# A two-layer hybrid backbone on one core: splits and a third diagonal buffer in the SSD pairs, value copies on VectorE between mLSTM heads, and a final norm applied tile by tile

## The chip, the cores and the metric

The kernel runs on one core of a Trainium2 chip. The time is that of one execution on the device, in microseconds. TensorE (PE) does matmuls and transposes, ScalarE (ACT) activations and copies, VectorE (DVE) elementwise work, scans and reductions, GpSimd (POOL) elementwise work and masks (affine selections), and SyncE (SP) issues DMAs. ScalarE issues some DMAs too. Each engine works off its own program in order, and engines meet through semaphores.

## The reference

One sample of 512 latent tokens and 256 context tokens, 1024 features, two layers, all in float32. Layer 0 runs gated linear attention (GLA, 4 heads) and Mamba-2 SSD (16 heads of 64 values, 128 states) beside each other; layer 1 runs a bidirectional mLSTM (4 heads of 512) in column-major grid order. Each layer ends with a SwiGLU FFN, and a final RMSNorm follows. Cut to what matters here:

```python
# SSD, both directions; per head h, chunks of 64, scalar decay
y, ... = bidir_scan(ch, bh * dt[0], bh * dt[1], xh, log_a[0], log_a[1], ...)
y = y + xh * d_skip ;  y = y * silu(z) ;  y = rmsnorm(y per group) ;  x += gate * (y @ w_out)

# mLSTM, per head and direction
s = einsum('bhid,bhjd->bhij', qc, kc) * exp(log_d - m_row)
num = einsum('bhij,bhje->bhie', s, vc) + w_inter * einsum('bhid,bhde->bhie', qc, c0)
h = num / max(abs(den), exp(-m_row))
hs = layernorm_nobias(h_f + flip(h_b)) ;  out = (hs + skip * xc) * silu(z)

# end
out = x * rsqrt(mean(x * x) + eps) * final_norm
```

## The kernel before

Activations lie transposed: `xT[P, 8, 768]` holds 8 tiles of 128 features by 768 tokens (512 latent, then 256 context; in layer 1 from the mLSTM on only the latent ones). A matmul of a weight tile with the activations is three matmuls of split float32 numbers, high times high, high times low, low times high. `weight_segments` orders all weight tiles in one line; they go through a ring of four buffers. SyncE loads a tile of 512 KB (`load`, L583), GpSimd splits it (`split`, L695 to L704) into `w_hi` and `w_lo`, TensorE multiplies (`tile_products`, L865; `project_unit`, L881), and `mm_done`, `evac` and `w_split` count the tiles. Results lie in PSUM: eight banks of 512 words, two of them a slot of 768.

*SSD stage* (around segments `out0` and `out1`). The 16 heads go in 8 pairs. For each head SyncE broadcasts two rows of cumulated decays to all partitions (`load_rows`, L618, a ring of two, 768 KB) and six rows for the context part. GpSimd selects the backward diagonal blocks into `Db` (L722; two buffers of 768 words, the one of head h is free when head h - 2 has been added up, `fb_done`), then the forward ones into `Dm` (L730; four buffers, two of them over `act_hi`). ScalarE takes exponentials (`decays_of`, `diagonal_decays`, `backward_decays`), and VectorE's `head_weights` (L2521) does, for head h: `exponents(h + 1)`, the context product `Dx` (L2550), the two sums of forward and backward blocks (L2533, L2536), the multiplication of `Dm` with the scores `cb` (L2539), and after an odd head the output of the pair before (L2556). TensorE's `pair_products` (L1184) multiplies the weights of two heads with the values; within it stands `context_decays` of the next odd head (L1160). Heads 0 to 7 use group 0's scores, heads 8 to 15 group 1's: TensorE computes seven pieces of them (`group_piece`, L1091), four ahead of pair 3's products and three behind them (L1213 to L1235), and ScalarE copies them to `cb` and `cbx` (`group_copy`, L1832) after head 8's decays, in the order of `SECOND` (L357). The first four weight tiles of `out1` are split by GpSimd after the selections of heads 5, 7, 9 and 11 (L733).

*mLSTM heads* (L1481 to L1537 on TensorE). In each head TensorE computes the outputs from `vt` and `Wf` (L1516), then the next head's stabiliser rows (`stabiliser_rows`, L1449) and values (`value`, L1432): four tiles of `xm`, each in two pieces of four and two 128x128 products, which go alternately to banks 2 and 3, so that piece i needs the copy of piece i - 2. Behind them stands the mean over features (L1526), then the next head's scores (`scores_of`, L1458). ScalarE copies the outputs to `hh`, takes the next head's exponentials (`weights`, L2066) and then copies the eight value pieces to `vt` (`head_value_copies`, L2054), with the load of the next `xm` tile behind each second one (ring of two). VectorE, meanwhile, adds the maxima (`weight_exponents`, L2740), sums `hh` over its four tiles (L2820, L2823) and waits for the mean (L2827).

*End.* Segment `down12` is the last: 8 tiles, each added to `xT` (L2482), squared by ScalarE (L1597) and summed (L2234). Then follow the sums over features (L814), the root (L1585), the reciprocal and a diagonal matrix (L2228, L2229), its spreading to all partitions by TensorE (L820), `fin` = x times `final_norm` times that (L2863, 8 instructions), 32 transposes into two banks (L1566), 8 copies to `obuf` (L2137), and four stores of 512 KB from ScalarE's queue (L2140), each as soon as its 128 tokens are complete.

## Time and profile before

| | |
|---|---|
| time, 3 runs | median 2545.46 us (2544.45 to 2546.82) |
| profiled execution | 2540.74 us, its span 2539.0 us |
| VectorE, ScalarE, GpSimd busy over the span | 56%, 25%, 42% |
| granted TensorE clock, mean | 0.966 of full |
| instructions | 33404 |

The profile page divides the span into 40 slices; in those of the SSD stage TensorE's busy share falls from 9 tenths to 7, and the granted clock with it:

```
PE   5999999999877989999999989999998999999997
PEclk8999999999888999999999999999999999999999
```

One slice is 63.5 us, so slices 11 to 13, where the shares are lower, are 635 to 825 us. A timeline row gives the start in the span, the duration, engine, line, operation, destination and sources, and in brackets how long the engine idled before it and who released it. Matmuls in float32 appear as two instructions each. The mLSTM heads lie between 1796 and 2105 us, the end from 2490 us on.

### The profile page before, as it was taken

How to read it: one execution, taken by the hardware profiler on the slowest of the kernel's cores; microseconds unless marked ns; L12 is line 12 of the kernel's file. 1: busy time of each engine (PE TensorE's matmuls, PEld its weight loads, DVE VectorE, ACT ScalarE, POOL GpSimd, SP SyncE). 2: the span in 40 equal slices, each digit the busy share in tenths (PEclk: the TensorE clock that was granted, in tenths of full speed). 3: DMA queues.
4: the chain of work that ended last, by engine and by line, in shares of the span. 5: the costliest groups of instructions: out<-in, count | busy, mean ns of one | idle time of the engine just before them, and what ended most of it. 6: DMA issues, size and time to landing. Idle time of an engine off the chain costs nothing.

```text
span 2539.0 us, 33404 instructions
## 1 busy us (share of the span) xinstructions
PE 2377.8 (94%) x12133; PEld 1882.9 (74%) x12133; DVE 1426.8 (56%) x2455; ACT 635.4 (25%) x1042; POOL 1073.3 (42%) x815
## 2 busy tenths in 40 slices
PE   5999999999877989999999989999998999999997
PEld 3887888887534878888888878876555457888886
DVE  4574778775586257778886646644366555111113
ACT  3202354433684131000000133133312302201001
POOL 2362343344362424464454344444211034666663
PEclk8999999999888999999999999999999999999999
DMA  7652342354430234343444213354233112333332
GB/s 273 216 175 83 98 144 73 116 173 150 163 114 13 84 66 117 100 133 102 129 117 116 79 46 122 122 164 141 75 96 108 35 53 83 97 94 99 92 95 71
DMA packets 390135, 280.98 MB, mean 111 GB/s; under 512 B 31106, under 2 KB 355228, under 8 KB 390012
## 3 DMA queue, kind: packets, MB, share of 16 engines
q1 hardware_dynamic: 333644, 201.51, 27.2%
q10 hardware_dynamic: 56368, 77.81, 9.0%
q8 instruction: 80, 1.31, 0.2%
q14 instruction: 43, 0.35, 0.0%
HBM read 237.21 MB, written 42.07 MB: 110 GB/s over the span
## 4 chain that ended last, share of the span: by engine, by line
PE 60%; DVE 5%; ACT 2%; issue 1%; DMA 1%; POOL 1%; DVEq 0%; ACTq 0%; POOLq 0%; SPq 0%
PE PS L869 43%; PE PS L1516 3%; PE PS L1359 3%; PE PS L1371 3%; PE PS L1468 2%; PE PS L820 1%; PE PS L1442 1%; DVE xcr L2300 1%; PE PS L1427 1%; PE PS L814 1%; PE PS L878 1%; DMA xmr<-xm_d 1%; PE PS L1314 0%; DVE hh L2851 0%; DMA w_raw<-in_ffn_w 0%
## 5 line engine op out<-in xcount | busy, mean ns | idle before, releaser
L700 POOL TENSOR_TENSOR w_hi<-w_raw,ones 128x128 fp32r<-128x128 f32 x244 | 160.9, 659 | 1269.2 <-DMA w_raw<-in_ffn_w 438.3
L703 POOL TENSOR_TENSOR w_lo<-w_raw,w_hi 128x1024 fp32r<-128x1024 f32 (+1 forms) x244 | 590.1, 2419 | 20.4
L869 PE MATMUL PS<-act_hi,w_hi 128*128 128x512 f32 (+1 forms) x1824 | 540.7, 362 | 29.1 <-DVE act_lo L2259 11.5
L869 PE MATMUL PS<-act_hi,w_lo 128*128 128x512 f32 (+1 forms) x1824 | 524.7, 353 | 0.0
L869 PE MATMUL PS<-act_lo,w_hi 128*128 128x512 f32 (+1 forms) x1824 | 521.4, 352 | 0.0
L869 PEld LDWEIGHTS PS<-act_hi,w_hi 128*128 128x128 f32 x1824 | 297.3, 192 | 78.5 <-issue 24.2
L869 PEld LDWEIGHTS PS<-act_lo,w_hi 128*128 128x128 f32 x1824 | 295.5, 191 | 48.3
L869 PEld LDWEIGHTS PS<-act_hi,w_lo 128*128 128x128 f32 x1824 | 295.5, 191 | 47.0
L2202 DVE SCALAR_TENSOR_TENSOR mf_acc<-mf_ring,cs,mf_acc 128x128 f32<-128x128 f32 x784 | 268.1, 417 | 2.0
L701 POOL TENSOR_SCALAR w_hi<-w_raw 128x896 fp32r<-128x896 f32 (+1 forms) x244 | 246.1, 1009 | 0.0
L2482 DVE SCALAR_TENSOR_TENSOR xT<-PS,modv,xT 128x512 f32<-128x512 f32 (+1 forms) x120 | 74.9, 657 | 236.2 <-PE PS L869 208.8
L2611 DVE TENSOR_TENSOR fhp<-fsg,PS 128x768 f32<-128x768 f32 (+1 forms) x44 | 36.1, 821 | 237.1 <-PE PS L869 211.5
L869 PE MATMUL PS<-hid_hi,w_hi 128*128 128x512 f32 (+1 forms) x528 | 163.2, 363 | 0.0
L869 PE MATMUL PS<-hid_hi,w_lo 128*128 128x512 f32 (+1 forms) x528 | 160.8, 359 | 0.0
L869 PE MATMUL PS<-hid_lo,w_hi 128*128 128x512 f32 (+1 forms) x528 | 160.5, 358 | 0.0
L1949 ACT ACTIVATE fsg<-PS 128x768 f32<-128x768 f32 (+1 forms) x44 | 31.1, 707 | 423.9 <-PE PS L869 423.8
L943 PE MATMUL PS<-act_hi,w_hi 128*128 128x512 f32 x448 | 121.6, 352 | 0.7 <-ACT stage L1708 0.7
L943 PE MATMUL PS<-act_hi,w_lo 128*128 128x512 f32 x448 | 116.4, 341 | 0.0
L943 PE MATMUL PS<-act_lo,w_hi 128*128 128x512 f32 x448 | 115.8, 340 | 0.0
L1952 ACT ACTIVATE hid_hi<-fhp 128x768 f32 (+1 forms) x44 | 32.6, 741 | 298.2 <-DVE fhp L2611 298.2
L869 PEld LDWEIGHTS PS<-hid_lo,w_hi 128*128 128x128 f32 x528 | 87.3, 188 | 16.4
L869 PEld LDWEIGHTS PS<-hid_hi,w_lo 128*128 128x128 f32 x528 | 87.4, 189 | 16.1
(348 smaller groups left out, 3605.1 us busy)
## 6 DMA issues: line engine op xcount, KB each, us to landing
w_raw<-in_ffn_w SPq DMA_DIRECT2D x120, 512.0 KB, 3.9
mf_ring<-in_w_mod SPq DMA_DIRECT2D x56, 512.0 KB, 4.0
w_raw<-in_a_w_in SPq DMA_DIRECT2D x44, 512.0 KB, 4.0
proj<-stage ACTq DMA_DIRECT2D x44, 384.0 KB, 4.0
w_raw<-in_b_w_up SPq DMA_DIRECT2D x32, 512.0 KB, 4.6
m_ring<-in_w_mod SPq DMA_DIRECT2D x12, 1024.0 KB, 8.2
rows<-g_d SPq DMA_DIRECT2D x16, 768.0 KB
m_raw<-in_w_mod SPq DMA_DIRECT2D x4, 2048.0 KB, 12.6
```

Source lines behind the costliest of these rows:

```text
L700: pool.tensor_tensor(w_hi[:, s, 0], w_raw[:, s, 0], ones[:], ALU.mult)
L701: pool.tensor_scalar(w_hi[:, s, 1:kt], w_raw[:, s, 1:kt], 1.0, 1.0, ALU.mult, ALU.mult).then_inc(w_hi_done, 1)
L703: pool.tensor_tensor(w_lo[:, s, 0:kt], w_raw[:, s, 0:kt], w_hi[:, s, 0:kt].bitcast(F32), ALU.subtract).then_inc(w_split, 1)
L869: last = pe.matmul(to[:, c0:c1], w[:, s, k, :], x[:, k, c0:c1], start=k == 0 and w is w_hi and x is hi, stop=k == kt - 1 and w is w_lo)
L943: last = pe.matmul(slot((n + 1) % 2)[:, c0:c1], w[:, n % RING, k, :], x[:, k, c0:c1], start=k == 0 and w is w_hi and x is act_hi, stop=k = ...
L1359: last = pe.matmul(bank(Z_BANK[j]), w[:, j % RING, k, :], x[:, k, 0:LAT], start=k == 0 and w is w_hi and x is act_hi, stop=k == KD - 1 and ...
L1371: last = pe.matmul(out, w[:, s, k, :], head_act(x, h, t), start=k == 0 and w is w_hi and x is act_hi, stop=k == KD - 1 and w is w_lo)
L1468: last = pe.matmul(bank(SCORE_BANKS[i]), xch[:, t, c * P:c * P + P], qp[:, t], start=t == 0, stop=t == 3)
L1516: last = pe.matmul(bank(OUT_BANKS[t]), vt[:, c, t * P:t * P + P], Wf[:, c], start=i == 0, stop=i == 5)
L2202: ins = dve.scalar_tensor_tensor(acc, mf_ring[:, s % 2, k], c, acc, ALU.mult, ALU.add)
L2482: ins = dve.scalar_tensor_tensor(x, y, g, x, ALU.mult, ALU.add)
L2611: dve.tensor_tensor(fhp[:, i, 0:n], fsg[:, i, 0:n], slot(s)[:, 0:n], ALU.mult).then_inc(evac, 2)
```

## The change

In the SSD stage: `Db` gets a third buffer, over `act_hi`; the backward selection of head h waits for head h - 3, and that of head 2 for out0's last product. The four splits go to heads 1, 2 and 3. All seven pieces of group 1 stand ahead of pair 3's products, in a new order. In the mLSTM stage: VectorE copies the values of heads 1 to 3, one tile ahead of its sums over `hh` and three behind them, and ScalarE's loads of `xm` move into `weights`. At the end: the weights of `final_norm` are multiplied in as each tile is done, half of the transposes stand behind tile 5 of `down12`, the reciprocal root is applied as a scale per token after the transposes, by ScalarE to the second half and by VectorE to the first, and SyncE issues the stores. New semaphore names lie on old semaphores. The diff, cut:

```diff
-        SECOND = (0, 1, 4, 5, 2, 3, 6)
+        SECOND = (0, 1, 4, 5, 6, 2, 3)
-        Db = sb("Db", [P, 2, T], offset=30720)
+        Db = [sb(f"Db{i}", [P, T], offset=30720 + 4 * T * i) for i in range(2)]
+        Db += [nc.alloc_sbuf_tensor_at("Db2", [P, T], F32, offset=act_hi_at + 8 * DM)]
...
-        fin = sb("fin", [P, KD, LAT], offset=24576)
-        obuf = sb("obuf", [P, 4, D], offset=43008)
+        fin = nc.alloc_sbuf_tensor_at("fin", [P, KD, LAT], F32, offset=zst_at)
+        obuf = nc.alloc_sbuf_tensor_at("obuf", [P, 4, D], F32, offset=act_hi_at)
@@ SyncE, at its end
+            for t in range(4):
+                sp.wait_ge(out_put, 5 + t)
+                sp.wait_ge(half_scaled, HALF0 + t + 1)
+                sp.dma_start(out[0, t * P:t * P + P, :], obuf[:, t]).then_inc(out_st[t % 2], 16)
@@ GpSimd
-                        if h >= 2:
-                            pool.wait_ge(fb_done, h - 1)
-                        pool.affine_select(out=diagonals(Db[:, h % 2], 0, 6, P), ...
+                        if h == 2:
+                            pool.wait_ge(mm_done, n0)
+                        elif h >= 3:
+                            pool.wait_ge(fb_done, h - 2)
+                        pool.affine_select(out=diagonals(Db[h % 3][:], 0, 6, P), ...
-                        if h == 2:
-                            pool.wait_ge(mm_done, n0)
...
-                        if h in (5, 7, 9, 11):
-                            split(n0 // RING, (h - 5) // 2, kt)
+                        if h in (1, 2, 3):
+                            for s in ((0, 1), (2,), (3,))[h - 1]:
+                                split(n0 // RING, s, kt)
@@ TensorE
+                    if name == "down12":
+                        last_tiles(name, kt, hi, lo, n, ready, ready0)
+                        return
...
+            def last_tiles(name, kt, hi, lo, n, ready, ready0):
+                r = segs[name][0] // RING + 1
+                for s in range(RING):
+                    project_unit(name, r, s, kt, hi, lo, n, ready, ready0)
+                    if s == 1:
+                        final_transposes(0, (0, 1, 2, 3))
...
                 if p == 3:
-                    for i in SECOND[0:4]:
+                    for i in SECOND:
                         group_piece(1, i)
...
                 elif p == 3:
-                    pair_products(p)
-                    for i in SECOND[4:7]:
-                        group_piece(1, i)
-                    context_decays(8)
+                    pair_products(p, lambda: context_decays(8))
...
+            def final_transposes(half, quarters):
+                pe.wait_ge(fin_ready, 4 * half + quarters[-1] + 1)
+                if half:
+                    pe.wait_ge(out_put, 4)
+                for t in range(4):
+                    for q in quarters:
+                        last = pe.transpose(bank(1 + 2 * t)[:, q * P:q * P + P], fin[:, 4 * half + q, t * P:t * P + P], ident[:])
+                    if quarters[-1] == 3:
+                        last.then_inc(out_tr, 1)
...
+            final_transposes(1, (0, 1, 2))
             pe.wait_ge(evac, segs["end"][0])
-            rstd_products(nacc, LAT, 3)
...
+            rstd_sums(nacc, LAT, 3)
+            final_transposes(1, (3,))
@@ ScalarE
+                    if name == "final" and k == 4:
+                        for t in range(4):
+                            act.wait_ge(out_tr, t + 1)
+                            act.activation(obuf[:, t, 0:512], bank(1 + 2 * t), ACT.Copy).then_inc(out_put, 1)
...
+            def next_xm(h, t):
+                if h and 4 * h + t + 2 < 16:
+                    act.wait_ge(qv_mm, QV_MM0 + 12 * h + 6 + 2 * t)
+                    load_xm(4 * h + t + 2)
@@ ScalarE, weights(h): next_xm(h, d) behind each direction's exponentials, next_xm(h, 2), next_xm(h, 3) at its end
...
                     weights(h + 1)
-                    head_value_copies(h + 1)
...
+            act.wait_ge(diag_done, rstds[0])
+            for t in range(4):
+                act.wait_ge(out_tr, 5 + t)
+                act.activation(obuf[:, t, 512:1024], bank(1 + 2 * t), ACT.Copy, scale=rcol[:, 0, t:t + 1]).then_inc(out_put, 1)
@@ VectorE
+            def final_weight(k):
+                dve.wait_ge(evac, segs["down12"][0] + k + 1)
+                dve.tensor_scalar(fin[:, k], xT[:, k, 0:LAT], par("final_norm", k), None, ALU.mult).then_inc(fin_ready, 1)
...
+            def value_copies(h, t):
+                f = 12 * h + 4 + 2 * t
+                for c0, c1 in ((0, 4), (4, 6)):
+                    dve.wait_ge(qv_mm, QV_MM0 + f + 1)
+                    dve.tensor_copy(vt[:, c0:c1, t * P:t * P + P], bank(2 + f % 2, ...)...).then_inc(val_put, 1)
+                    f += 1
...
                     weight_exponents(h + 1)
+                    value_copies(h + 1, 0)
...
                 dve.drain().then_inc(hs_rdy, 1)
+                if h + 1 < ML_HEADS:
+                    for t in range(1, 4):
+                        value_copies(h + 1, t)
                 dve.wait_ge(mean_mm, h + 1)
...
-            norm_sums("final", LAT)
-            for k in range(KD):
-                dve.scalar_tensor_tensor(fin[:, k], xT[:, k, 0:LAT], par("final_norm", k), slot(3)[:, 0:LAT], ALU.mult, ALU.mult).then_inc(fin_ready, 1)
+            add_norm_square(NORMS.index("final"), KD - 1, LAT)
+            dve.drain().then_inc(sum_done, 1)
+            final_weight(KD - 1)
+            rstds[0] += 1
+            dve.wait_ge(std_done, rstds[0])
+            dve.reciprocal(rcol[:, 0, 0:4], rcol[:, 0, 0:4]).then_inc(diag_done, 1)
+            dve.wait_ge(diag_done, rstds[0])
+            for t in range(4):
+                dve.wait_ge(out_put, t + 1)
+                dve.tensor_scalar(obuf[:, t, 0:512], obuf[:, t, 0:512], rcol[:, 0, t:t + 1], None, ALU.mult).then_inc(half_scaled, 1)
```

## Rows read from the trace of the kernel before

**Rows 1.** The page, busy time of TensorE: us, share of the span, instructions.
```profile
PE 2377.8 (94%) x12133; PEld 1882.9 (74%) x12133; DVE 1426.8 (56%) x2455; ACT 635.4 (25%) x1042; POOL 1073.3 (42%) x815
```

**Rows 2.** Waits of TensorE: who waited for whom, us in total, times, longest.
```profile
PE PS L1442 <- ACT vt L2060: 14.4, 3, 4.8
```

**Rows 3.** Timeline, from mLSTM head 0 to head 1: TensorE and VectorE.
```profile
1820.17 1.98 PE L1456 MATMUL PS<-negM,ident 8*128 8x512 f32 x4
1822.08 1.60 PE L1442 MATMUL PS<-bdv,xmr 128*128 128x128 f32 x12
1822.19 0.69 DVE L2746 TENSOR_TENSOR Wb<-PS,ucol 128x512 f32<-128x512 f32 x1 [0.17 <-PE PS L1456]
1823.51 1.73 DVE L2823 TENSOR_TENSOR mtmp<-mtmp,hh 128x512 f32<-128x512 f32 x2
1828.48 5.73 PE L1442 MATMUL PS<-bdv,xmr 128*128 128x128 f32 x24 [4.79 <-ACT vt L2060]
1835.90 1.02 PE L1526 MATMUL PS<-mtmp,ones 128*128 128x512 f32 x2
1836.96 2.87 DVE L2827 SCALAR_TENSOR_TENSOR hh<-PS,hh 128x512 f32<-128x512 f32 x4 [11.72 <-PE PS L1526]
```

**Rows 4.** Busy time by engine in one SSD pair, clock and DMA share.
```profile
701.25:717.39 16.14, 12.15 (x48) 4.78 (x48) 15.28 (x12) 12.82 (x37) 13.55 (x10) 0.90 0.38 125
```

**Rows 5.** Timeline of the end: last residual, sums, a last transpose group, copies, stores.
```profile
2516.52 0.75 DVE L2482 SCALAR_TENSOR_TENSOR xT<-PS,modv,xT 128x512 f32<-128x512 f32 x1 [2.85 <-PE PS L869]
2518.93 1.02 PE L814 MATMUL PS<-ones,nacc 128*128 128x1 f32 x8 [2.52 <-DVEq L2240]
2531.47 0.35 ACTq L2140 DMA_DIRECT2D out_y<-obuf  x1
2532.62 0.63 PE L1566 MATMUL PS<-ident,fin 128*128 128x128 f32 x4 [0.40 <-ACT obuf L2137]
2534.84 0.34 ACTq L2140 DMA_DIRECT2D out_y<-obuf  x1
```

**Rows 6.** DMA traffic from 2500 to 2540 us, one number for each us.
```profile
GB/s 22 242 130 0 0 0 0 0 0 0 0 0 0 0 0 0 0 0 0 0 16 0 0 0 0 0 0 0 0 0 0 0 283 401 385 418 406 213 0 0
```

**Rows 7.** VectorE's copies out of PSUM at line 2156: ns least, median, most.
```profile
L2156 DVE COPY xT<-PS x12: 691/692/693, 18.6 to 27.1; 128x512 f32<-128x512 f32 x12
```

**Rows 8.** Timeline of the SSD pairs, VectorE, GpSimd, ScalarE and TensorE.
```profile
701.08 2.83 DVE L2539 TENSOR_TENSOR Dm<-Dm,cb 128x2560 f32<-128x2560 f32 x1
707.44 2.68 POOL L703 TENSOR_TENSOR w_lo<-w_raw,w_hi 128x1024 fp32r<-128x1024 f32 x1
707.82 2.59 DVE L2536 TENSOR_TENSOR Dm<-Dm,Db 128x256 f32<-128x256 f32 x1
710.44 2.83 DVE L2539 TENSOR_TENSOR Dm<-Dm,cb 128x2560 f32<-128x2560 f32 x1
710.61 3.37 POOL L722 TENSOR_SCALAR_AFFINE_SELECT Db<-rows 128x768 f32<-128x768 f32 x1 [0.50 <-DVE Dm L2536]
714.02 0.70 ACT L1869 ACTIVATE Db<-Db,nb 128x128 f32<-128x128 f32 x2 [3.32 <-POOL Db L722]
714.02 1.10 DVE L2519 TENSOR_TENSOR Db<-Db,nb 128x512 f32<-128x512 f32 x1 [0.76 <-POOL Db L722]
719.36 1.45 PE L1191 MATMUL PS<-xt,skip 128*128 128x512 f32 x4
728.07 0.60 ACT L1840 ACTIVATE cb<-PS 128x512 f32<-128x512 f32 x1 [5.17 <-PE PS L1111]
730.52 2.83 DVE L2539 TENSOR_TENSOR Dm<-Dm,cb 128x2560 f32<-128x2560 f32 x1 [7.22 <-ACT cbx L1840]
753.77 2.83 DVE L2539 TENSOR_TENSOR Dm<-Dm,cb 128x2560 f32<-128x2560 f32 x1
760.54 2.83 DVE L2539 TENSOR_TENSOR Dm<-Dm,cb 128x2560 f32<-128x2560 f32 x1
767.03 2.82 DVE L2539 TENSOR_TENSOR Dm<-Dm,cb 128x2560 f32<-128x2560 f32 x1
```

68 lines of the change are left out of this document (37 added, 31 removed).

## The prediction

> **What bounds the kernel now.** I read the page's busy shares first, then the waits by engine, then time-ordered instructions of the three places that the diff touches. TensorE is busy for 94% of the span [rows 1], so a wait costs time where it stops TensorE, or where it moves what TensorE gets next. The three places differ.
>
> In the mLSTM stage TensorE waits for ScalarE's copies of the value products three times, 14.4 us together [rows 2]. One turn from head to head is in [rows 3]: the stabiliser rows start at 1820.17, the first two value products at 1822.08, the third at 1828.48 after 4.79 us of idling, the mean product at 1835.90. It takes 15.7 us. The reader is to see that ScalarE was not slow: it works off the next head's exponentials first, because they stand ahead of the copies in its program.
>
> In the SSD pair loop TensorE is the idle one. In the 16.14 us of one pair VectorE is busy for 15.28, ScalarE for 12.82, GpSimd for 13.55 [rows 4]. So the loop runs at VectorE's pace, and what lengthens VectorE's own instructions counts.
>
> At the end TensorE has nothing left: from the last residual at 2516.52 to the end of the span, 22.5 us, a serial chain runs: sums, root, reciprocal, spreading, eight products for `fin`, transposes, eight copies, four stores [rows 5].
>
> **The end of the program.** Now: the last store is issued at 2534.84 and the span ends at 2539.0, so 4.2 us after it. The four stores of 512 KB are one stream at about 400 GB/s, from about 2532.3 to 2537.5 [rows 6]: 5.2 us, begun 0.9 us behind the first issue at 2531.47, and 1.5 us follow it.
> After: the weights of `final_norm` go on tile by tile (VectorE idles 2.85 us before each residual [rows 5], and one such product is under 0.75 us: hidden), the first half's 16 transposes stand behind tile 5, and the reciprocal root is applied at the very end as a scale. Four transposes take 0.63 us in the last row of that kind [rows 5], so 16 of them put about 2.2 us (16/4 x 0.63 = 2.5, less the tails that overlap) into the stage that TensorE bounds. ScalarE's four copies of half 0 lie beside tile 6. From the last residual on, in the old clock: 12 transposes (1.6 us) lie in the wait for the last square; sums at 2518.93 and root as before; reciprocal done at about 2520.5; the last four transposes run beside the root. Then ScalarE's four scaled copies at about 0.55 us each (such a copy shows 0.60 [rows 8], back to back a little less, an estimate), VectorE's four multiplications beside them: stores issued from 2521.3 to 2522.9. The stream then sets the end: 2521.3 + 0.9 + 5.2 + 1.5 = 2528.9. With the 2.2 us that is 2531.1, against 2539.0: **-8 us**. It cannot be below -11 (the spread product, `fin` and half of the copies are all there is to take), nor above -5, where the four stores from SyncE would come one by one at their 4.2 us latency in part. Moving the stores from ScalarE's queue to SyncE's puts them behind weight loads only, and DMA is almost silent from 2503 to 2531 [rows 6].
>
> **The turn between mLSTM heads.** ScalarE loses 24 copies, VectorE gets them. The only price of such a copy on VectorE is the copy of 128x512 out of PSUM at the start of the program, 0.69 us [rows 7]; that of 128x256 I estimate at 0.4. Counted from the stabiliser rows' start: value products 0 and 1 end at 3.5 (1.60 us for twelve instructions, 0.133 each; a pair of pieces is those twelve [rows 3]). VectorE finishes the second diagonal block at 2.7 and copies at 3.1 and 3.8, until 4.2. TensorE does pieces 2 and 3 from 3.8 to 5.4. VectorE now does its three sums over `hh`, 2.4 us (0.7, and 1.73 for two [rows 3]), until 6.6; the next copies come behind them, until 7.8. Pieces 4 and 5: 7.4 to 9.0. Copies until 9.7, pieces 6 and 7 until 11.0, mean product at 11.0. Now it is 15.7, so 4.7 less.
> Two loads of `xm` are moved: the one for piece 6 is issued after the second group of exponentials, about 6 us from the start, and has 3.4 us until piece 6; I take off 0.2 for a load that comes late: 4.5 a turn, three turns: **-13.5 us**. VectorE's 4.4 us of copies cover themselves: it idles 11.72 us before the mean now [rows 3]. Behind the mean product everything keeps its distance: scores wait for the last copy, which ends while the mean product runs. From both sides: with no copy late, TensorE's own work is 1.9 + 4 x 1.6 = 8.3 us, a gain of 7.4 a turn; if each pair waits for a full round of VectorE behind its sums, 2.
>
> **The SSD pairs.** Four edits have one answer, VectorE's time per head. The multiplications of `Dm` by `cb` are its beat [rows 8]. Without a weight split on GpSimd the beat is 6.77 us (753.77 to 760.54) and 6.49 (760.54 to 767.03); with one it is 9.36 (701.08 to 710.44). In that pair the sum of the short diagonal block, L2536, took 2.59 us where it lay against the split's 2.68 us: it ended 0.3 us behind it. So a split costs 2.6 us.
> *Splits.* Those at heads 5, 7 and 11 each cost 2.6, the one at head 9 fell into VectorE's wait of 7.22 us for `cb` [rows 8] and cost nothing. At heads 1 to 3 they meet out0's last tiles, where TensorE bounds, and the wait for head 4's rows; one of them may put head 3's selection back by some tenths, but head 4's rows arrive no sooner for that. So -7.8.
> *Third buffer.* ScalarE waits 3.32 us in a split pair for the even head's backward selection, VectorE 0.76 [rows 8]. The selection took 3.37 us because it started right with a multiplication of 2.83. With a third buffer it may start a head earlier. But without the splits ScalarE's own 12.8 us per pair [rows 4] and VectorE's 12.5 (13.26 less such a wait) are all but equal, so the pair goes from 13.26 to about 12.8: 0.45 x 5 pairs, -2.2. It cannot gain more than the 0.76 a pair, 3.8.
> *Second group.* Now TensorE goes into pair 3 at 719.36 and computes the last three pieces behind it; ScalarE waits 5.17 us for them and VectorE then 7.22 for the copies [rows 8]. After, TensorE waits before pair 3 for ScalarE's first copy (about 2 us), does the three pieces, and pair 3 starts some 5 us late against its head. `cb` is there 4 us sooner, but head 9's context product now stands behind pair 3 on TensorE, and VectorE waits for that instead: of the gain, nothing reaches head 9's multiplication, and I put this edit at +1.2 (pair 3's products take TensorE from 719.36 to about 727, 7.6 us, and with transposes and the context product behind them they end that much later than ScalarE's chain would). From -4 to +4.
> Also the second head's backward selection now waits for out0's last product, since its buffer lies over `act_hi`; the forward one, behind it, ends later by one selection, and ScalarE asks for it about then: 0 to +0.7, I take 0.
> Sum, with 0.8 for VectorE instructions that meet a selection at new places: -7.8 - 2.2 + 1.2 + 0.8 = **-8 us**, between -2 and -14.
>
> A rule of the Trainium skill speaks against this part. The row first: L2536 stood still until the split was done, and L722 until the multiplication was [rows 8]. The Trainium skill, "SBUF — State Buffer", section "Who interferes with whom", says that a VectorE instruction with two SBUF inputs and a GpSimd instruction that reads SBUF exclude each other, and whichever is second blocks. The trace agrees. By that rule a selection that may start when its rows land, and not with a multiplication, blocks VectorE where it used to be the one blocked: rival (a) below, which gives 2524 where the rows of the undisturbed pair give 2516.
>
> **The sum.** -8 - 13.5 - 8 = -29.5 us. The profiled execution took 2540.74 us (span 2539.0 and 1.7 around it), so 2511.2. The median of the three timed runs is 2545.46, 4.7 above it; I carry the difference over to the median: **2516.0 us**.
>
> **Rivals.**
> (a) The shared port takes back the third buffer and more. For: every selection now may start beside VectorE's short sums; the part of L722 outside the multiplication is 0.7 us [rows 8], and with the two forward ones that is some 2 us a head. At 0.8 us a head more in the ten heads from 5 on: +8, SSD at 0, total -21.5, 2524. Against: in the pair without a split such meetings cost only 0.3 us. 15%.
> (b) VectorE becomes the bound of the turn: its sums and drain are ahead of six of eight copies. If each turn gains 2 us and not 4.5: -22, 2523.5. For: the chain above has TensorE idle twice, 2.0 and 0.4 us. Against: the idle 11.72. 12%.
> (c) More comes: SSD -13 (the wait of 7.22 is saved in whole) and turns at -5.5: 2508. 10%.
> (d) Slower. TensorE's granted clock. In the pair loop it is 0.90 of full on average [rows 4], so part of that stretch ran at 1.2 GHz and not at 2.4, and TensorE idles there between products. If the value stage of a turn (three short bursts with idle between, in place of one long wait) left it at 1.2 for 12 us of full-speed work behind it, these would take 24, 36 more in three turns: -29.5 + 36 = +6.5, 2552. It decides from 30 us of such work. Against: the idle time there gets shorter in all. 2%.
> (e) The change does not do what it says: the third buffer's selection still waits, now for its rows (the ring of two row buffers is unchanged), and the reordering cancels: SSD -5, 2519; within my forecast's own range. 9%.
> My forecast has 52%.
>
> **How the numbers follow.** The time is that of the forecast. The range for 8 in 10 reaches to (a) and (b) and most of (c): 2509 to 2526. A measurement of this kernel tells about 0.2%, 5 us, from no change: faster by more than that has every case but (d) and some accident of code loading or order: 0.94, same 0.03, slower 0.03.
>
> **What would show it.** Turns: ScalarE as the releaser of value products gone, stabiliser row to mean product 11.2 us. End: the last store issued 6 to 7 us after the last residual, not 18; 16 transposes ahead of tile 6. SSD: the beat 6.0 to 6.8 in all heads from 4 on but 8 and 9, L2536 never at 2.6, no wait of 7 us before head 8's multiplication but one of 3 to 4 us on a context product of head 9. Wrong would be: a beat still near 9, a turn above 13.5, or TensorE's clock at half for long in either stage.

## The result and the profile after

The changed kernel takes 2509.8 us in the median of 4 runs (2505.1 to 2518.9), the one before 2545.0 in as many runs beside it (2541.9 to 2546.8): ratio 0.9876, 95% interval 0.9841 to 0.9911. The forecast was 2516.0. The profiled execution took 2505.09 us, its span 2503.4, 35.6 less than the profiled one before; the forecast made against that one was 29.5 less. One run of one experiment (two_buffers) took 9134.6 us, at a granted clock of 1.00 and for a reason that no trace shows, and is left out of that kernel's median and ratio.

TensorE is as busy as it was [rows 1]:

```profile
PE 2354.4 (94%) x12131; PEld 1869.7 (75%) x12131; DVE 1446.5 (58%) x2482; ACT 622.7 (25%) x1018; POOL 1053.7 (42%) x815
```

**The turns.** Waits of TensorE: who waited for whom, total, times, longest. in the three turns ScalarE is gone as releaser of value products [rows 2], and VectorE stands there with half of the time:

```profile
PE PS L1482 <- DVE vt L2804: 7.5, 9, 1.6
PE PS L828 <- DVEq L2895: 3.2, 1, 3.2
PE PS L1482 <- DMA xmr<-xm_d: 0.9, 1, 0.9
```

The same turn as in [rows 3], timeline of TensorE and VectorE in the changed kernel:

```profile
1804.83 1.98 PE L1496 MATMUL PS<-negM,ident 8*128 8x512 f32 x4
1806.74 1.60 PE L1482 MATMUL PS<-bdv,xmr 128*128 128x128 f32 x12
1807.93 1.02 DVE L2804 COPY vt<-PS 128x512 f32<-128x512 f32 x2 [0.40 <-PE PS L1482]
1808.77 1.58 PE L1482 MATMUL PS<-bdv,xmr 128*128 128x128 f32 x12 [0.43 <-DVE vt L2804]
1808.87 0.68 DVE L2879 TENSOR_TENSOR mtmp<-hh 128x512 f32<-128x512 f32 x1
1809.59 1.42 DVE L2882 TENSOR_TENSOR mtmp<-mtmp,hh 128x512 f32<-128x512 f32 x2
1811.15 1.02 DVE L2804 COPY vt<-PS 128x512 f32<-128x512 f32 x2
1811.98 1.58 PE L1482 MATMUL PS<-bdv,xmr 128*128 128x128 f32 x12 [1.64 <-DVE vt L2804]
1813.99 1.58 PE L1482 MATMUL PS<-bdv,xmr 128*128 128x128 f32 x12 [0.43 <-DVE vt L2804]
1815.40 1.02 PE L1572 MATMUL PS<-mtmp,ones 128*128 128x512 f32 x2
```

From the stabiliser rows to the mean product it is 1815.40 - 1804.83 = 10.57 us, and the same in the other two turns; before it was 15.73, 15.59 and 15.60. So 15.2 us in three turns. The listed waits fell by only 6.9 us (14.4 to 7.5), since a row that joins many products hides the short pauses between them: the 24 products at 1828.48 in [rows 3] take 5.73 us, where twelve take 1.60, so 2.5 us of pauses lie inside that row.

**The end.** Timeline from the first half's transposes on:

```profile
2480.46 1.91 PE L1300 MATMUL PS<-ident,fin 128*128 128x128 f32 x16
2480.66 0.75 DVE L2527 SCALAR_TENSOR_TENSOR xT<-PS,modv,xT 128x512 f32<-128x512 f32 x1 [2.19 <-PE PS L893]
2486.61 0.75 DVE L2527 SCALAR_TENSOR_TENSOR xT<-PS,modv,xT 128x512 f32<-128x512 f32 x1 [4.08 <-PE PS L893]
2490.82 0.75 DVE L2527 SCALAR_TENSOR_TENSOR xT<-PS,modv,xT 128x512 f32<-128x512 f32 x1 [2.33 <-PE PS L893]
2493.22 1.02 PE L828 MATMUL PS<-ones,nacc 128*128 128x1 f32 x8 [1.14 <-DVEq L2924]
2494.11 0.64 PE L1300 MATMUL PS<-ident,fin 128*128 128x128 f32 x4
2494.79 2.42 ACT L2187 ACTIVATE obuf<-PS,rcol 128x512 f32<-128x512 f32 x4 [0.24 <-DVE rcol L2928]
2494.80 1.68 DVE L2932 TENSOR_SCALAR obuf<-obuf,rcol 128x512 f32<-128x512 f32 x4
2495.51 2.90 SPq L682 DMA_DIRECT2D out_y<-obuf  x4
```

From the last residual to the end of the span 2503.4 - 2490.82 = 12.6 us, where it was 22.5 [rows 5]. DMA traffic from 2463 to 2503 us shows the stores at the same 400 GB/s as before [rows 6]:

```profile
GB/s 0 94 306 305 81 0 138 253 2 0 118 252 23 0 0 0 0 0 0 0 0 0 0 0 16 0 0 0 0 0 0 0 0 258 414 397 393 406 225 12
```

**The SSD pairs.** One pair by engine, as in [rows 4] (us, then PE, PEld, DVE, ACT, POOL busy, clock, DMA share, GB/s):

```profile
695.47:708.63 13.16, 9.50 (x45) 3.81 (x45) 12.30 (x11) 12.77 (x38) 6.80 (x6) 1.00 0.50 154
```

It takes 13.16 us where it took 16.14, and GpSimd has half of its work gone. Timeline rows that answer to [rows 8]:

```profile
671.09 2.67 POOL L716 TENSOR_TENSOR w_lo<-w_raw,w_hi 128x1024 fp32r<-128x1024 f32 x1
671.47 2.58 DVE L2587 TENSOR_TENSOR Dm<-Dm,Db 128x256 f32<-128x256 f32 x1
689.09 2.83 DVE L2590 TENSOR_TENSOR Dm<-Dm,cb 128x2560 f32<-128x2560 f32 x1
690.04 2.59 POOL L737 TENSOR_SCALAR_AFFINE_SELECT Db<-rows 128x768 f32<-128x768 f32 x1 [7.32 <-DMA xrow<-cross_d]
692.67 0.69 DVE L2570 TENSOR_TENSOR Db<-Db,nb 128x512 f32<-128x512 f32 x1 [0.76 <-POOL Db L737]
714.00 1.15 PE L1141 MATMUL PS<-rdiag,bct 128*128 128x512 f32 x2 [1.96 <-ACT cb L1882]
714.96 3.58 PE L1135 MATMUL PS<-rdiag,bct 128*128 128x512 f32 x4
719.30 2.83 DVE L2590 TENSOR_TENSOR Dm<-Dm,cb 128x2560 f32<-128x2560 f32 x1 [4.78 <-ACT cb L1882]
728.30 1.23 DVE L2601 TENSOR_TENSOR Dx<-PS,cbx 128x1024 f32<-128x1024 f32 x1 [4.09 <-PE PS L1195]
730.62 2.83 DVE L2590 TENSOR_TENSOR Dm<-Dm,cb 128x2560 f32<-128x2560 f32 x1
736.90 0.93 POOL L737 TENSOR_SCALAR_AFFINE_SELECT Db<-rows 128x768 f32<-128x768 f32 x1 [7.19 <-DMA xrow<-cross_d]
737.14 3.36 DVE L2590 TENSOR_TENSOR Dm<-Dm,cb 128x2560 f32<-128x2560 f32 x1
```

The reader is to see five things. The split now holds L2587 up at head 2. The backward selection of head 6 waits for a transfer (the last of its rows), starts inside the multiplication of head 4, and VectorE waits the same 0.76 us for it as before. And head 8's multiplication waits 4.8 us in place of 7.2, while head 9 then waits 4.1 us for its context product. Ahead of both, four products of group 1's pieces take 3.58 us behind TensorE's wait of 1.96, where the same four take 1.98 in six_last at a granted clock of 1.00; here it was 0.50 from 715 to 717 us. And the backward selection of head 12 starts 0.24 us ahead of the multiplication of head 10, which then takes 3.36 us in place of 2.83.

### The profile page after: what moved, and what is told of

Read it like the earlier page. It is cut to its first block, busy times and chain, and to the rows that moved or that the text cites. A ratio compares the mean times of both kernels' runs of the same rounds, so it can differ in the third digit from the quotient of the medians.

```text
span 2503.4 us, 33402 instructions
## 1 busy us (share of the span) xinstructions
PE 2354.4 (94%) x12131; PEld 1869.7 (75%) x12131; DVE 1446.5 (58%) x2482; ACT 622.7 (25%) x1018; POOL 1053.7 (42%) x815
## 4 chain that ended last, share of the span: by engine, by line
PE 60%; DVE 6%; issue 1%; POOL 1%; DMA 1%; ACT 1%; ACTq 0%; DVEq 0%; POOLq 0%; SPq 0%
PE PS L893 44%; PE PS L1562 3%; PE PS L1391 3%; PE PS L1403 3%; PE PS L1514 2%; PE PS L834 1%; PE PS L1482 1%; PE PS L828 1%; PE PS L1463 1%; PE PS L902 1%; DVE xcr L2345 1%; PE PS L1346 0%; DVE hh L2913 0%; DVE hh L2911 0%; PE PS L1222 0%
## 5 line engine op out<-in xcount | busy, mean ns | idle before, releaser
L713 POOL TENSOR_TENSOR w_hi<-w_raw,ones 128x128 fp32r<-128x128 f32 x244 | 151.6, 621 | 1264.0 <-DMA w_raw<-in_ffn_w 451.2
L893 PE MATMUL PS<-act_hi,w_hi 128*128 128x512 f32 (+1 forms) x1824 | 539.0, 361 | 26.6 <-DVE act_lo L2304 11.0
L893 PEld LDWEIGHTS PS<-act_hi,w_hi 128*128 128x128 f32 x1824 | 296.1, 192 | 75.7 <-issue 21.5
## 6 DMA issues: line engine op xcount, KB each, us to landing
m_raw<-in_w_mod SPq DMA_DIRECT2D x4, 2048.0 KB, 12.4
```

What stands on the lines that cost most here:

```text
L713: pool.tensor_tensor(w_hi[:, s, 0], w_raw[:, s, 0], ones[:], ALU.mult)
L893: last = pe.matmul(to[:, c0:c1], w[:, s, k, :], x[:, k, c0:c1], start=k == 0 and w is w_hi and x is hi, stop=k == kt - 1 and w is w_lo)
```

## The experiments

Times of stages come from each run's own profile, one for each kernel. The ratios of the experiments are to the kernel before as it ran beside each group of experiments (medians of 2542.0 to 2543.1 us), not to the 2545.0 of the first line. For SSD the yardstick is the distance from the start of head 1's multiplication by `cb` to that of head 15's. Heads 7 to 9 hold the switch to group 1.

| kernel | time, median (runs) | ratio, 95% interval | heads 1-15 | 3-7 | 7-9 | 9-15 |
|---|---|---|---|---|---|---|
| before | 2545.0 (4) | | 117.9 | 32.3 | 20.4 | 41.2 |
| changed | 2509.8 (4) | 0.9876 (0.9841 to 0.9911) | 111.6 | 26.1 | 22.0 | 38.3 |
| changed, again | 2508.3 (6) | 0.9868 (0.9839 to 0.9897) | 114.1 | 26.4 | 22.0 | 40.4 |
| splits_only | 2530.5 (10) | 0.9955 (0.9939 to 0.9972) | 111.4 | 26.3 | 21.5 | 38.1 |
| end_only | 2533.5 (10) | 0.9970 (0.9953 to 0.9986) | 117.7 | 32.3 | 20.4 | 41.2 |
| turns_only | 2529.3 (7) | 0.9941 (0.9924 to 0.9959) | 117.9 | 32.3 | 20.4 | 41.2 |
| two_buffers | 2503.0 (3) | 0.9850 (0.9800 to 0.9900) | 111.3 | 26.6 | 21.9 | 38.1 |
| late_splits | 2516.2 (4) | 0.9877 (0.9831 to 0.9924) | 117.5 | 32.8 | 18.8 | 40.8 |
| old_group | 2512.6 (4) | 0.9874 (0.9832 to 0.9916) | 114.1 | 28.3 | 22.3 | 38.1 |
| six_last | 2510.6 (4) | 0.9872 (0.9843 to 0.9900) | 110.8 | 26.2 | 19.1 | 40.4 |
| six_last_ctx | 2506.9 (4) | 0.9849 (0.9818 to 0.9879) | 107.5 | 26.4 | 15.9 | 39.8 |
| early_rows | 2510.6 (6) | 0.9869 (0.9839 to 0.9899) | 109.3 | 26.7 | 20.5 | 38.6 |
| combo | 2504.8 (6) | 0.9858 (0.9829 to 0.9887) | 107.4 | 26.4 | 15.9 | 39.8 |
| combo_two | 2505.6 (6) | 0.9860 (0.9831 to 0.9888) | 105.8 | 26.3 | 15.8 | 39.8 |

**two_buffers.** Undoes the third buffer.

```diff
-        Db += [nc.alloc_sbuf_tensor_at("Db2", [P, T], F32, offset=act_hi_at + 8 * DM)]
...
+                        if h >= 2:
+                            pool.wait_ge(fb_done, h - 1)
...
-                        elif h >= 3:
-                            pool.wait_ge(fb_done, h - 2)
   (every Db[h % 3] is Db[h % 2]; the wait for mm_done is back behind the backward selection)
```

> The changed kernel with two backward buffers in place of three (the wait for the head before the last is back). Yardstick of all runs on the SSD stage: from the start of head 1's multiplication by cb to that of head 15's, 117.9 us before the change, 111.6 after. Theory A (the forecast on record): the third buffer is worth 0.45 us a pair, so 113.8. Theory B: it is worth nothing, because a backward selection waits for its rows, and their load waits for ScalarE, which must have read the rows of two heads earlier: 111.6 +- 0.5, and the selections of heads 6 to 12 start at the same distance from the multiplications as in the changed kernel. Theory C: it costs (selections now lie against VectorE's short sums): 110.5 or less.

Measured 111.3, so the size is that of theory B: the third buffer is worth nothing (heads 3 to 15 take 86.6 us without it and 86.5 with it). Its mechanism is only half right. The first row is the backward selection of head 6, the others group its 16 selections by what ended the idle time before them (us, times):

```profile
689.76 3.38 POOL L734 TENSOR_SCALAR_AFFINE_SELECT Db<-rows 128x768 f32<-128x768 f32 x1 [2.01 <-DVE Dm L2586]
...
  DMA xrow<-cross_d: 32.5, 10
  DVE Dm L2586: 10.3, 6
```

With two buffers six selections wait for VectorE's sum and not for rows. They start 0.2 us behind the start of the multiplication that follows the sum. With three, those of heads 6 to 9 start 0.4 to 1.7 us into it, when the rows are there. Both end behind it. Later the third buffer does let some go sooner: those of heads 12, 13 and 15 start 0.1 to 0.35 us ahead of a multiplication, and the multiplications of heads 10, 11 and 13 then take 3.36, 3.36 and 3.47 us in place of 2.83 [the last two rows above]. So they save VectorE one wait of 0.76 us and four stretched `exponents` (0.95 us in place of 0.69), and cost it 1.7. With two buffers one multiplication is so stretched, by 0.5 us (head 1).

**late_splits.** Undoes the move of the splits.

```diff
-                        if h in (1, 2, 3):
-                            for s in ((0, 1), (2,), (3,))[h - 1]:
-                                split(n0 // RING, s, kt)
+                        if h in (5, 7, 9, 11):
+                            split(n0 // RING, (h - 5) // 2, kt)
```

> The changed kernel with the four weight splits of out1 back behind the selections of heads 5, 7, 9 and 11. Theory A: each of three costs 2.6 us again and the early places cost nothing: 111.6 + 7.8 = 119.4. Theory B: three cost 2.6 each, but the early places cost 1.2 (heads 1 to 3 took 25.2 us from head 1's multiplication to head 3's, 24.0 before): 118.2. Theory C: with three buffers a split is hidden in part, since the selection behind it can wait: 115 or less.

117.5: the splits cost 5.9 of the yardstick, nearest to theory B (118.2) and against C. The two stretches with splits take 32.8 and 40.8 us, as before the change; the third buffer hides none of it. Heads 1 to 3 take 25.1 us here too, so the early splits alone do not explain the 1.2 us more that heads 1 to 3 show after the change; splits_only, which has them and nothing else, takes 25.5 there. Heads 7 to 9 take 18.8 us here against 20.4 in the kernel before, which has the same splits: with the splits late, the new order gains 1.6. A split now meets another instruction, to the same price, here `exponents`:

```profile
692.93 2.88 DVE L2569 TENSOR_TENSOR Db<-Db,nb 128x512 f32<-128x512 f32 x1
...
692.91 2.35 POOL L716 TENSOR_TENSOR w_lo<-w_raw,w_hi 128x1024 fp32r<-128x1024 f32 x1
```

**old_group.** Undoes the order of group 1.

```diff
-        SECOND = (0, 1, 4, 5, 6, 2, 3)
+        SECOND = (0, 1, 4, 5, 2, 3, 6)
...
-                    for i in SECOND:
+                    for i in SECOND[0:4]:
                         group_piece(1, i)
...
-                    pair_products(p, lambda: context_decays(8))
+                    pair_products(p)
+                    for i in SECOND[4:7]:
+                        group_piece(1, i)
+                    context_decays(8)
```

> The changed kernel with the old handling of group 1's scores: four pieces ahead of pair 3's products, three and both context products behind. Theory A: the new order costs 1.2 us: 110.4. Theory B, from the two traces: head 7's to head 9's multiplication took 22.0 us after the change and 20.4 before, so 1.6 less: 110.0. Theory C: the new order gains, and the loss is from the missing cover of the split at head 9: 112 or more.

114.1 would speak for theory C, but the 2.2 us more lie at heads 3 to 7, ahead of the edit, where TensorE's clock was low for longer in this run (last section). Heads 7 to 9, where the edit is, take 22.3 us against 22.0: the order of the change is worth 0.3, neither A's nor B's loss. Inside, head 8 comes 3.9 us sooner with the new order (10.7 behind head 7, against 14.6) and head 9 3.6 later (11.3 behind head 8, against 7.7). One thing stands in the way of this comparison: in the changed kernel the four products behind TensorE's wait of 1.96 us ran at a low clock and took 1.6 us longer [the row at 714.96 above]. In early_rows below, which has the new order and not this drop, heads 7 to 9 take 20.5. And splits_only shows 1.1 us of loss there with the old order. So theory C is right in part: the loss at heads 7 to 9 goes with the missing cover for the split at head 9.

**splits_only.** The kernel before, with the splits moved and nothing else (the edit of late_splits, reversed).

> The kernel before, with only the four splits moved to heads 1, 2 and 3. Theory A: 117.9 - 7.8 = 110.1. Theory B: 117.9 - 8.4 (the beats of the three heads fell from 9.35 to 6.5) + 1.2 for the early places = 110.7, that is 0.9 us less than with the whole SSD part, because the rest of that part costs. Theory C: without the third buffer the even heads' selections still wait for VectorE, and only half comes: 114. The whole time falls by the same amount: 2538 by A and B.

111.4: the splits alone give all of the SSD gain, 6.5 us, though not all of theory B's 7.2. Heads 3 to 7 and 9 to 15 gain 9.0, heads 7 to 9 give 1.1 back and heads 1 to 3 1.5. Head 8 waits for its scores still longer than before [rows 8]:

```profile
723.73 2.83 DVE L2540 TENSOR_TENSOR Dm<-Dm,cb 128x2560 f32<-128x2560 f32 x1 [8.50 <-ACT cbx L1841]
```

**end_only** and **turns_only.** The kernel before, with one part of the change each, word for word: for end_only `last_tiles`, `final_transposes`, `final_weight`, the scaled copies and the stores from SyncE; for turns_only `value_copies`, `next_xm` and the waits on `val_put`.

> The kernel before, with the end-of-program part alone. Theory A (the forecast): from the last residual to the end of the span 12.4 us where it was 22.5, 16 transposes of 2.2 us ahead of tile 6, so -8 in all, about 2535 in the median. Theory B: the gain needs nothing of the other parts, and the profile shows the same 12.6 and 2.2 as the whole change. Theory C: a part of it is lost in the rest of the program (the final transposes hold up the last weight tiles' products further): -5, 2538.

2533.5, ratio 0.9970: 7.6 us, theories A and B. From the last residual (2517.89) to the end of the span (2529.6) it is 11.7 us, 0.9 less than in the whole change: the first store is issued 4.7 us behind the residual in both, and the stores end sooner here.

> The kernel before, with VectorE's value copies in the mLSTM turns alone. Theory A (the forecast): each turn takes 11.2 us from stabiliser rows to mean product, -13.5 in all. Theory B, from the trace of the changed kernel: 10.6 each, -15.2, about 2528; and where GpSimd's split behind head 3 meets VectorE's third sum of squares, 2.1 us of that are lost again (the wait of TensorE for the sum is 3.2 us in place of 1.1). Theory C: the turns only show a gain that heads 1 to 3 pay back (scores wait for the last copies): the distance from one mean product to the next falls by less than 5 us.

2529.3, ratio 0.9941: 15.0 us. The turns take 10.57 us each, and the wait for the sum of squares behind head 3 is 3.1 us: theory B. C's number is met and its reason is not: from one mean product to the next it is 80.4 and 81.9 us, 84.2 and 85.0 before, so 3.8 and 3.1 less. Between the first two TensorE's clock was 0.91 in one window of 20 us (1854 to 1874), where it was 1.00 at the same instructions of the whole change (1838 to 1858), and between the others it waited 1.8 us once for a sum of VectorE's, as it does in end_only, which has the old turns. In the first profile of the whole change the same distances are 79.0 and 79.9, so 5.2 and 5.1 less, and nothing is paid back; in the second they are 78.9 and 81.8. In the nine profiles with turns of 10.57 us the two distances add up to 158.9 to 164.1 us, 161.3 in the mean, in the three with the old turns to 168.8 to 172.0, 170.0 in the mean. So of the 10.0 us that two turns gain 8.7 are seen in the mean; that heads 1 to 3 never pay back is not shown.

The three ratios of single parts multiply to 0.9867; the whole change measured 0.9876 and 0.9868. The parts add up within their intervals of about 0.0016 each, and the third buffer and the new order, which no single part has, need not add anything.

**six_last.** The changed kernel, with `SECOND` as before and all seven pieces ahead of pair 3.

```diff
-        SECOND = (0, 1, 4, 5, 6, 2, 3)
+        SECOND = (0, 1, 4, 5, 2, 3, 6)
```

> The changed kernel with the old order of group 1's pieces (0, 1, 4, 5, 2, 3, 6), all seven still ahead of pair 3's products. In the changed kernel piece 6 stands ahead of 2 and 3 and waits 1.96 us for ScalarE's first copy, and these two behind it. Theory A: the order costs as much as that wait: head 8's multiplication and pair 3's products come 2.2 us earlier, and head 15's too; from head 1's to head 15's multiplication 109.4 us in place of 111.6. Theory B: pieces 2 and 3 wait for VectorE's output of pair 2 instead, at about the same time, and nothing changes: 111.6. Theory C: head 8 comes earlier, but ScalarE or GpSimd bound heads 9 to 15 and take it back: head 8 -2, head 15 within 0.5.

Head 8 comes 2.3 us sooner and heads 7 to 9 take 2.9 us less, theory A's mechanism; the piece that stands third from the end waits 0.33 us for VectorE in place of 1.96 for ScalarE, and its four products take 1.98 us, at full clock, where they took 3.58. Part of the 2.9 us is therefore the clock. The low clock followed the wait in three of the four profiles that have it (1.96 us), and in the five that have these products and not the wait they took 1.88 to 1.99 us:

```profile
711.55 1.98 PE L1135 MATMUL PS<-rdiag,bct 128*128 128x512 f32 x4 [0.33 <-DVE yT L2607]
714.23 1.45 PE L1215 MATMUL PS<-xt,skip 128*128 128x512 f32 x4
```

The yardstick shows 110.8 and not 109.4: heads 9 to 15 took 40.4 us, two more than in the first run of the changed kernel and as many as in its second. Theory C is not excluded by this run; the next one speaks against it.

**six_last_ctx.** In addition the context product of head 9 moves into pair 3's products.

```diff
                         between()
+                    if p == 3 and c == 3:
+                        context_decays(9)
...
-                if p == 3:
-                    context_decays(9)
```

> As six_last, and head 9's context product stands within pair 3's products, behind their fourth chunk, in place of behind the transposes that follow them. VectorE waited 4.1 us for it in the changed kernel. Theory A: VectorE's wait goes, head 9's multiplication follows ScalarE's exponentials at 6.5 to 7 us behind head 8's in place of 11.3, ScalarE's wait for pair 3 bounds head 10, and head 1 to head 15 takes 105 to 106. Theory B: the product waits for VectorE's context product of head 8 and holds up pair 3's last chunks, so head 10 comes as late as before: 109.4, as in six_last.

107.5, between A and B: VectorE's wait for the product is 0.3 us where it was 4.1 [the row at 728.30 above], and head 9 follows head 8 by 7.5 us in place of 11.3. Then head 10 needs 8.5, for pair 3's products end late against it (ScalarE waits 1.80 us for them), which is B's mechanism in part.

```profile
726.58 0.70 PE L1195 MATMUL PS<-xrow 6*128 6x512 f32 x2 [0.66 <-DVE Dx L2601]
```

**early_rows.** The memory of the third buffer goes to a third buffer of backward rows, with transfers of their own.

```diff
+        row_b = nc.alloc_sbuf_tensor_at("row_b", [P, T], F32, offset=act_hi_at + 8 * DM)
...
-                        sp.dma_start(rows[:, h % 2], src).then_inc(rows_in[h % 2], 16)
+                        sp.dma_start(rows[:, h % 2, 0], src).then_inc(rows_in[h % 2], 16)
...
+                        if h >= 4 and h + 1 < SSD_HEADS:
+                            load_back(h + 1)
...
-                        pool.wait_ge(rows_in[h % 2], ROWS_IN0 + 32 * (h // 2 + 1))
+                        pool.wait_ge(rb_in[RB[h]], back_count(h))
```

> The changed kernel with two backward buffers, and the memory of the third given to a third buffer for the backward rows, loaded by a transfer of their own one head ahead, so that a backward selection no longer waits for its rows. Theory A: the rows are what holds the selections; VectorE's wait of 0.76 us in every pair goes, and the beats of a pair fall from 13.2 us to ScalarE's 12.8: from head 1's to head 15's multiplication 109 to 110 us in place of 111.3. Theory B: the selections already come as soon as they help, and nothing changes: 111.3 +- 0.4. Theory C: selections that start early meet VectorE's short sums, or block the forward ones: 112 or more.

109.3, the size of theory A and not its mechanism. The pairs take as long as before: 26.7 us from head 3 to 7. Now ten selections wait for VectorE's sum, as in this row of head 7, and VectorE still waits 0.76 us in five of the pairs:

```profile
694.04 3.38 POOL L756 TENSOR_SCALAR_AFFINE_SELECT Db<-rows 128x768 f32<-128x768 f32 x1 [1.40 <-DVE Dm L2610]
...
713.76 1.88 PE L1157 MATMUL PS<-rdiag,bct 128*128 128x512 f32 x4
```

The 2 us come from head 3, which follows head 2 by 6.9 us in place of 8.3, and from heads 7 to 9 (20.5 us against 21.9 in two_buffers). The latter is the clock: the four products behind TensorE's wait of 1.97 us take 1.88 us here and 3.34 in two_buffers, where the granted clock was 0.50 from 717 to 719 us. So the selection is held twice: by its rows, and, about 1 us earlier, by the sum, which stands right ahead of the multiplication. One buffer more of either kind moves it only from one to the other. Both at once were not tried.

**combo** and **combo_two.** six_last_ctx with VectorE's sums set between its copies; combo_two with two buffers in addition.

```diff
                 for t in (2, 3):
+                    if h + 1 < ML_HEADS:
+                        value_copies(h + 1, t - 1)
                     dve.wait_ge(h_put, H_PUT0 + 4 * h + t + 1)
                     chain(dve.tensor_tensor(acc, acc, hh[:, t], ALU.add))
...
-                    for t in range(1, 4):
-                        value_copies(h + 1, t)
+                    value_copies(h + 1, 3)
```

> six_last_ctx with VectorE's sums over hh set between its value copies in the mLSTM turns (copy tile 0, sum, copy tile 1, sum, copy tile 2, sum, copy tile 3). Theory A: TensorE's wait of 1.64 us before the fifth piece goes, the last tile of xm, issued by ScalarE behind its exponentials, bounds pieces 6 and 7: a turn takes 9.3 us in place of 10.57, -3.8 in all. Theory B: it takes 8.8, since the transfer is in time. Theory C: the mean product, which needs the last sum, becomes the bound: 10.2. With SSD at 107.5 (as six_last_ctx) the span is some 7 to 8 us under the changed kernel's.

> combo with two backward buffers. If the third buffer is worth nothing here too: SSD 107.5 +- 0.5, the time that of combo. If the shorter SSD stage makes it useful: 108.5 to 110.

The turn takes 10.17 us: 0.4 less, a miss against A and B, and nearest to C's number, but not for C's reason. The transfer of `xm` is the next wait, and it comes for the third tile already:

```profile
1811.47 1.60 PE L1482 MATMUL PS<-bdv,xmr 128*128 128x128 f32 x12 [1.14 <-DMA xmr<-xm_d]
1813.57 1.58 PE L1482 MATMUL PS<-bdv,xmr 128*128 128x128 f32 x12 [0.50 <-DVE vt L2804]
```

SSD takes 107.4 and, with two buffers, 105.8, which is 1.2 less than was expected at least. The difference lies at heads 1 to 3 (25.4 and 23.9 us; why is not settled), and heads 3 to 15 take 82.0 in both: the third buffer is worth nothing here either. Both kernels have a lower median than the changed one (2504.8 and 2505.6 against 2508.3 beside them), but with six runs each from 2500.6 to 2514.2 the order among the three is not shown.

**after_again.** The changed kernel, unchanged.

> The changed kernel once more, unchanged, beside the others on one chip. All theories: about 2508 to 2510 in the median; SSD 111.6 +- 0.5 if TensorE's granted clock takes the same course, up to 3 more if it stays low longer; turns 10.57 each; 12.6 us from the last residual to the end. It tells what one profiled execution differs from another.

2508.3; the turns 10.57 each, the end 12.6. SSD 114.1, that is 2.5 more than the first time, within what was expected for a clock that stays low longer. It is the measure of how far two profiles of one kernel differ there.

## Why the prediction was right, point by point

Forecast 2516.0, measured 2509.8: inside the range of 2509 to 2526, 0.8 us above its lower end. Rival (c)'s 2508 is nearer than the forecast, but its reasons did not come: head 8's wait was not saved in whole, SSD gained 6.9 us and not 13, and a turn 5.1, between the 4.5 of the forecast and the 5.5 of (c). That the sum of the parts came out so close is in part luck, since errors of both signs lie in it.

**The end: right, and in its steps.** Forecast 12.4 us from the last residual to the end, measured 12.6; forecast 2.2 us for 16 transposes, measured 1.75 (the residual of tile 6 follows that of tile 5 by 5.95 us, that of tile 7 by 4.21, and end_only shows the same). The issues of the four stores lie from 4.7 to 7.6 us after the residual (2495.51 and 2.90 for the four; forecast 4.8 to 6.4), and the stream of four at 400 GB/s sets the end as forecast. Net -8.1 for -8.

**The turns: right mechanism, the size a little low.** Forecast 11.2 us a turn, measured 10.57. Pieces 2 and 3 started 3.94 us after the rows' start (forecast 3.8), 4 and 5 at 7.15 (7.4), 6 and 7 at 9.16 (9.4 by the forecast's steps), the mean product at 10.57 (11.0, and 0.2 for a late load). The terms mis-sized are VectorE's sums, 2.14 us and not 2.4, and its copies: two in 1.02, not 0.7 and 0.4 one after the other. Gain 15.2 for 13.5. Rival (b) falls: no turn gained only 2.

**SSD: the sum nearly right, from terms that were not.** Forecast -8, measured -6.3 by the yardstick (-6.9 counted from the end of out0's last product to head 15).
The step of the splits is right at its places: the steps to the multiplications of heads 4, 6 and 10, which follow the selections of heads 5, 7 and 11, fell from 9.36 us to 6.60, 6.78 and 6.52. But with them gone, heads 7 to 9 gave 1.1 us back (the new scores did not come sooner for it), and heads 1 to 3 up to 1.5, of which 0.7 is that the zero of the yardstick was late before. That term was -7.8 and is -6.5. The forecast said that L2536 is never at 2.6 again; at head 2 it took 2.58 [the row at 671.47], inside a stretch in which VectorE then waits for head 3's selection.
The step of the third buffer failed: "with a third buffer it may start a head earlier". It did not; its rows land 0.4 to 1.7 us behind the sum that it had waited for. -2.2 was forecast, 0 is measured (two_buffers, and again combo_two). That is rival (e)'s mechanism, which had 9%; its price of 3 us on the whole was about right for this term and wrong for the sum.
The second group: mechanism right, the wait of VectorE for head 9's context product (forecast 3 to 4 us, measured 4.1) and of TensorE before pair 3 (2, measured 1.96). The size was +1.2 and is -0.3, with 1.6 us of low clock in it that the forecast did not have.
The meetings, +0.8: seen, and larger. In the pair from 695.47 to 708.63 there is none: each of VectorE's sums of diagonal blocks took 0.69 or 0.41 us, the durations that they have alone. But the multiplications of heads 10, 11 and 13 were stretched by 1.7 us together (the second profile of the kernel shows three such, 1.7 us too, and the kernel before none), and two steps between heads took 7.06 and 7.16 us, beyond the 6.0 to 6.8 that the forecast had named. This is rival (a)'s mechanism, which the Trainium skill's rule ("SBUF — State Buffer", section "Who interferes with whom") carried, at three heads and not at ten. At the others it falls: the third buffer's selection still starts inside the multiplication, and then it is GpSimd that stands still. The trace agrees with the rule itself, in 671.47 and 737.14 above and in the next point.

**What the forecast did not have.** Behind head 3 VectorE's third sum of squares meets GpSimd's split of a weight tile. Timeline of the changed kernel, and of the kernel before:

```profile
2053.65 4.98 DVE L2894 TENSOR_TENSOR mtmp<-mtmp 128x512 f32<-128x512 f32 x3
2055.43 2.65 POOL L716 TENSOR_TENSOR w_lo<-w_raw,w_hi 128x1024 fp32r<-128x1024 f32 x1
```

```profile
2084.41 2.89 DVE L2832 TENSOR_TENSOR mtmp<-mtmp 128x512 f32<-128x512 f32 x3
...
2086.85 2.66 POOL L703 TENSOR_TENSOR w_lo<-w_raw,w_hi 128x1024 fp32r<-128x1024 f32 x1
```

The split begins 1.78 us after the first sum does, not 2.44, and the third sum waits for its end: TensorE waits 3.2 us in place of 1.1. This +2.1 is in the time of the changed kernel. It is not due to the turns: end_only has it (3.2), old_group and combo have not.

**The sum against the profile.** SSD -6.9, turns -15.2, end -8.1, collision +2.1 make -28.1; measured were -35.6. The rest, 7.5, lies where both kernels are the same: -3.0 ahead of the SSD stage, -3.8 from there to 956 us, nearly all of it between 925 and 948, -1.7 until the mLSTM stage, and +1 in small pieces. In the first two places the profiled execution of the kernel before had been slow: 8 and 13 of the 13 other profiles are quicker there. In the third 6 are quicker and 7 slower, so there the profile of the changed kernel was the quick one. The forecast took one profile as its base. Whether these accidents also explain the distance of the medians, from 2516.0 to 2509.8, is not shown: both profiled executions were 4 to 5 us under their medians, and the interval of the ratio allows a gain from 22.6 to 40.5 us, so that 6.2 us are within the noise of four runs. By the timed runs, the parts alone give 7.6 + 15.0 + 11.4 = 34.0 us with an uncertainty of about 4 each (the ends of their intervals), and for the splits the traces show 6.5 to 7.1; where another 4 of their 11.4 would be is open, and the interval (7.1 to 15.5) does not demand it.

## What to carry to other kernels

A buffer more helps a stage only if what fills it also comes sooner: before costing it, follow the instruction's other wait, here the transfer of its rows, and ask how far behind the removed one it ends (about 1 us). Where it does come sooner, ask what it then meets. An engine whose copies stand behind other work in its program order can be relieved of them where another engine waits anyway, and the gain is then most of TensorE's wait (some 7.5 us a turn before, counting the short pauses, and 2.5 after). And a forecast made against one profiled execution inherits that execution's accidents: 7.5 us of the 36 between the two profiles here.

## What was not expected of the hardware

TensorE's granted clock falls in the SSD pairs in episodes that differ from run to run. Some cost a head about 2 us, as below, and some nothing that the steps show: splits_only had 0.74 from 730 to 740 us, the kernel before 0.66 from 750 to 760, and the steps there took their usual 6.8 us. Two runs of the changed kernel, windows 730 to 740 us; of the two rows the first is the first run, at full clock:

```profile
730.00:740.00 10.00, 7.47 (x30) 2.52 (x30) 9.90 (x9) 10.00 (x30) 0.93 (x1) 1.00 0.46 167
```

```profile
730.00:740.00 10.00, 8.54 (x21) 2.70 (x22) 9.90 (x9) 9.87 (x30) 0.96 (x1) 0.56 0.54 171
```

In the second, a mean of 0.56 means that half of full speed, 1.2 GHz and not 2.4, was granted for most of the window. TensorE had waited 1.46 us for a multiplication ahead of its products, in the first run 1.65, so the wait alone does not tell. Eight products take 3.68 us, then, and not 1.94, the pair ends late, the forward selection that waits for it moves, and the next head's backward selection with it, until VectorE waits for GpSimd and then for ScalarE:

```profile
733.25 3.68 PE L1222 MATMUL PS<-Dm,xtok 128*64 128x512 f32 x8 [1.46 <-DVE Dm L2590]
...
747.55 1.03 DVE L2570 TENSOR_TENSOR Db<-Db,nb 128x512 f32<-128x512 f32 x1 [0.91 <-POOL Db L737]
...
751.18 0.69 DVE L2584 TENSOR_TENSOR Dm<-Dm,Db 128x512 f32<-128x512 f32 x1 [1.47 <-ACT Db L1920]
```

Head 12 then follows head 11 by 9.3 us, in the first run by 7.1. The same episode lies in six_last (head 12, 8.6) and in old_group (head 6, 8.7). Hence the stretches of single heads, and not the yardstick alone, decide between kernels here.

Between 935 and 945 us the clock was 0.76 in the kernel before and 1.00 in the changed one at the same instructions, and TensorE's idle time there, for nothing that the profile shows, 5.2 and 2.6 us. The first multiplication by `cb` starts in the 13 other profiles between 3.9 us earlier and 4.0 later than in the kernel before, though all that stands ahead of the SSD stage is the same.
